# A two-block transformer kernel: the split weight rings whi and wlo placed 16 bytes lower in SBUF

## The chip, the cores and the metric

One core of a Trainium2 chip runs the whole program in one launch. The metric is the device time of that launch in microseconds (us). The kernel before was timed at 2585.36 us, the median of 3 runs (2585.33 to 2587.22).

## The reference

The reference computes two transformer blocks one after the other on 256 tokens of width 2048, in float32.

- First block: a position embedding is added to x; a modulation vector comes from silu(c) @ w_mod (2048 x 12288), also for a context; both x and the 256 context tokens are normalised, modulated and multiplied by w_in (2048 wide); gated linear attention runs in both directions, with the states of the context carried over; a 2-D Fourier mix runs beside it; both branches are read out (w_fourier_out, w_gla_out), gated and multiplied by w_out; then a squared-ReLU MLP, h @ w_mlp_in (2048 x 8192) and back by w_mlp_out.
- Second block: RMS norm, h @ w_in_2, three convolution and pooling mixers, w_out_2, a norm; then a gated convolution MLP with w_up_2 (2048 x 11264) and w_down_2 (5632 x 2048), and a last norm.

Nearly all arithmetic is in the matrix products with weights that come from HBM, some 540 MB in float32, each used once.

## The kernel before, in words

**Split products.** TensorE multiplies operands of type float32r. To keep float32 accuracy most weights w are split in two, whi (w rounded to float32r) and wlo (w minus whi), and so are the activations (hh and hl, mh and ml, ch and cl, dh and dl, oh and ol, yfh and yfl, all named "hi" and "lo" below). Each product of a 128 x 128 block of weights is three matmuls: hi times whi, hi times wlo, lo times whi.

**Staging.** SyncE loads weight slots of 128 x 2048 float32 (1 MB) into the ring `raw` (four slots, six while `raw2` is free). A slot gives two pieces of 128 x 1024. For each piece ScalarE copies raw to whi (`hi_piece`, L246, instruction at L254), VectorE subtracts to make wlo (`lo_piece`, L258, instruction at L263), and TensorE uses both. whi and wlo are rings of four pieces each; `STREAM` and `PIECE` give the order of slots and pieces, and semaphores count them: whi may be overwritten once `used` shows that TensorE is four pieces on, and TensorE waits for `lo_n`. The last two pieces of all go to `xh` and `xl` (128 x 2 x 1024 each), which lie elsewhere, so that they can be split before the ring is free.

**Two forms of a piece.** In `feature_piece` (L285, matmuls at L295, L297 and L299) the weights are the stationary operand, 128 x 128 at a time, and the moving operand is 256 tokens of an activation; a piece has 24 such matmuls. In `token_piece` (L304, matmuls at L315, L316 and L317) an activation block of 128 tokens is stationary and 512 columns of whi or wlo are moving; a piece has 12 matmuls, or 24 where the context is done with it. The last group of w_down_2 is written out at L2055 to L2057 in the same way; of its six pieces, the first four are in whi and wlo and the last two in xh and xl. `mm_lr` (L358, L367 to L369) has one piece with 64-column weights. Four groups at L352 use weights from raw without the split.

**Placement.** SBUF tensors lie one behind the other in each partition; an `overlay` gives several tensors the same region in turn. What matters for the change is where each operand begins, in bytes of a partition, modulo 128. Every matmul operand begins at a whole number of 512 bytes from the start of its tensor (256 in `mm_lr`), so these remainders hold for all of them.

| tensor | use in the matmuls | begins at, modulo 128 |
|---|---|---|
| whi | weights (feature), moving (token) | 16 |
| wlo | the same | 80 |
| hh, hl, mh, ml, ch, cl, oh, ol, yfh, yfl | moving (feature), stationary (token) | 32 |
| dh, dl | stationary (token, w_down_2) | 0 |
| xh, xl | moving (last two pieces) | 32 |
| raw, tmp | read by ScalarE and VectorE; raw is also the stationary operand at L352 | 0 |
| raw2 | as raw, for two slots of six while it is free | 32 |
| hf | moving at L352 | 32 |

hh begins at byte 109,472, mh at 142,240, oh at 191,904; hl, ml and ol, which follow them, at 125,856, 158,624 and 200,096. Each of the whi and wlo tensors has 16 columns (64 bytes) more than the ring needs; the ring begins 4 columns into it.

The lines that the diff touches are the two that allocate whi and wlo in `build`.

Of the kernel before, what the change touches and what calls it, by code (L numbers as in the profile page):

```python
# [4 lines left out]
P = 128  # L5
# [3 lines left out]
GC = 512  # L9
# [80 lines left out]
def build(nc, ins, out):  # L90
    f32, f32r, u32 = mybir.dt.float32, mybir.dt.float32r, mybir.dt.uint32
# [4 lines left out]
    with ctx:  # L96
        def sb(name, shape, dt=f32):
            return ctx.enter_context(nc.sbuf_tensor(name, shape, dt))
# [12 lines left out]


        raw = sb("raw", [P, NSLOT, 4 * GC])
        whi = sb("whi", [P, 8 * GC + 16], f32r)[:, 4:8 * GC + 4].rearrange("p (r n) -> p r n", r=4)
        wlo = sb("wlo", [P, 8 * GC + 16], f32r)[:, 4:8 * GC + 4].rearrange("p (r n) -> p r n", r=4)
        tmp = sb("tmp", [P, 2, 4 * NT])
        (mrow, cv, posc, macc, stage, _, posc2, sx, post) = overlay(
            "region_s", 8192,
# [2031 lines left out]
```

How the kernel before makes its waits and increments, by code:

```python
        def load(sp, st, name, slot, n=4, cols=4 * GC):  # L211
            for i in range(slot, slot + n):
                if PREV[st.k] is not None:
                    c = STREAM[PREV[st.k]]
                    before = STREAM[:PREV[st.k] + 1]
                    n_mod = before.count("m")
                    if c == "m" and n_mod <= EARLY:
                        sp.wait_ge(S["mod_used"], n_mod)
                    elif c == "m":
                        sp.wait_ge(S["mod_acc"], n_mod - EARLY)
                    elif c == "f":
                        sp.wait_ge(S["f_used"], before.count("f"))
                    else:
                        sp.wait_ge(S["lo_n"], 2 * before.count("d") + before.count("l"))
                sp.dma_start(raw_slot(st.k)[:, 0:cols], ins[name][i]).then_inc(raw_full[RING[st.k]], 16)
                st.k += 1
# [7 lines left out]
        def slot_in(eng, k):  # L235
            eng.wait_ge(raw_full[RING[k]], 16 * FILLS[k])
# [9 lines left out]
        def hi_piece(act, st):  # L246
            k, j = PIECE[st.p]
            if j == 0:
                slot_in(act, k)
            if st.p >= len(PIECE) - 2:
                act.wait_ge(S["fid_ok"], FT // 4)
            elif st.p >= 4:
                act.wait_ge(S["used"], st.p - 3)
            nc.scalar.activation(ring(whi, xh, st.p), raw_slot(k)[:, 2 * GC * j:2 * GC * (j + 1)], ACT.Copy)\
                .then_inc(S["hi_n"], 1)
            st.p += 1
# [24 lines left out]
        def group_done(eng, st):  # L281
            eng.wait_ge(S["used"], st.e)
```

## Time and profile before

| | us |
|---|---|
| median of 3 runs | 2585.36 |
| the profiled execution | 2586.47 |
| its span on the core | 2584.7 |
| TensorE busy in it | 2533.3 |
| VectorE busy | 1669.4 |
| ScalarE busy | 1141.4 |

The span is what the hardware profiler saw of the core's instructions; the execution's own time is 1.8 us longer, outside it. The profiled execution is 1.1 us above the median. Matmuls are pipelined: each lasts longer in the profile than the distance from its start to the start of the next, so what a matmul costs is read from starts, as first start and last start over the number between them, and not from the mean duration of one.

### The profile page before, as it was taken

To read this page: it belongs to the slowest core of one execution; us is meant where nothing else is said; L and a number is where in the kernel's file an instruction comes from. 1 tells how busy PE (TensorE), PEld (TensorE's weight loads), DVE (VectorE), ACT (ScalarE), POOL (GpSimd) and SP (SyncE) were. 2 spreads that over 40 slices of the span, in tenths; PEclk is the share of its full clock that TensorE was granted. 3 is DMA by queue.
4 is the path that set the end of the run, shared out by engine and by line. 5 is a ranking of instruction groups with operands and counts; after the bars stand their busy time and mean duration, and the time that the engine had idled before them with its cause. 6 is when DMAs were issued, how large, how long until landed. Compare 5 with 4: busy or idle time off the path is not lost.

```text
span 2584.7 us, 42715 instructions
## 1 busy us (share of the span) xinstructions
PE 2533.3 (98%) x18976; PEld 2379.1 (92%) x18976; DVE 1669.4 (65%) x2016; ACT 1141.4 (44%) x1311; POOL 11.2 (0%) x24
## 2 busy tenths in 40 slices
PE   6999999999998999999999999999999999999998
PEld 3688799999998999999999999999899889988997
DVE  5366666677787755555545579776667557764775
ACT  3422555544445434434434552054445444443554
POOL 0000000000000000000000000000000000000000
PEclk8999999999999999999999999999999999999999
DMA  9966565587875755555555555455455555555543
GB/s 401 371 241 231 213 225 198 212 300 289 303 288 195 289 184 196 184 192 194 184 193 193 183 181 178 147 180 177 149 181 196 195 182 193 192 184 194 186 175 128
DMA packets 77224, 547.90 MB, mean 212 GB/s; under 512 B 8848, under 2 KB 8976, under 8 KB 12272
## 3 DMA queue, kind: packets, MB, share of 16 engines
q1 hardware_dynamic: 74304, 533.53, 56.9%
q0 software_dynamic: 2448, 11.14, 1.1%
q8 instruction: 149, 2.44, 0.4%
q10 hardware_dynamic: 288, 0.50, 0.1%
q14 instruction: 35, 0.29, 0.0%
HBM read 539.90 MB, written 5.24 MB: 211 GB/s over the span
## 4 chain that ended last, share of the span: by engine, by line
PE 96%; DMA 1%; DVE 1%; ACT 1%; issue 1%; SPq 0%; DVEq 0%; ACTq 0%
PE acc L295 23%; PE acc L299 23%; PE acc L297 23%; PE acc L315 5%; PE acc L316 5%; PE acc L317 5%; PE acc L352 4%; DMA raw<-in_w_mod 1%; PE mp L382 1%; PE mp L315 1%; PE mp L317 1%; PE mp L316 1%; PE mp L441 0%; DVE macc L426 0%; PE mp L1857 0%
## 5 line engine op out<-in xcount | busy, mean ns | idle before, releaser
L263 DVE TENSOR_TENSOR wlo<-raw,whi 128x1024 fp32r<-128x1024 f32 x779 | 942.3, 1223 | 679.4 <-ACT whi L254 678.1
L254 ACT ACTIVATE whi<-raw 128x1024 fp32r<-128x1024 f32 x779 | 818.3, 1058 | 1180.9 <-PE acc L299 881.3
L295 PE MATMUL acc<-hh,whi 128*128 128x256 f32 x3360 | 940.1, 280 | 5.5 <-issue 5.5
L299 PE MATMUL acc<-hl,whi 128*128 128x256 f32 x3360 | 941.6, 280 | 0.0
L297 PE MATMUL acc<-hh,wlo 128*128 128x256 f32 x3360 | 934.7, 278 | 0.0
L295 PEld LDWEIGHTS acc<-hh,whi 128*128 128x128 f32 x3360 | 635.5, 189 | 10.6 <-issue 8.9
L299 PEld LDWEIGHTS acc<-hl,whi 128*128 128x128 f32 x3360 | 632.0, 188 | 0.0
L297 PEld LDWEIGHTS acc<-hh,wlo 128*128 128x128 f32 x3360 | 630.3, 188 | 0.5
L299 PE MATMUL acc<-ml,whi 128*128 128x256 f32 x1536 | 430.4, 280 | 0.0
L295 PE MATMUL acc<-mh,whi 128*128 128x256 f32 x1536 | 426.6, 278 | 0.0
L297 PE MATMUL acc<-mh,wlo 128*128 128x256 f32 x1536 | 426.5, 278 | 0.0
L295 PEld LDWEIGHTS acc<-mh,whi 128*128 128x128 f32 x1536 | 290.5, 189 | 0.3 <-issue 0.2
L299 PEld LDWEIGHTS acc<-ml,whi 128*128 128x128 f32 x1536 | 288.4, 188 | 0.0
L297 PEld LDWEIGHTS acc<-mh,wlo 128*128 128x128 f32 x1536 | 287.3, 187 | 0.1
L426 DVE SCALAR_TENSOR_TENSOR macc<-raw,csl,macc 128x512 f32<-128x512 f32 x240 | 180.2, 751 | 8.0
L316 PE MATMUL acc<-wlo,dh 128*128 128x512 f32 x328 | 129.9, 396 | 0.0
L317 PE MATMUL acc<-whi,dl 128*128 128x512 f32 x328 | 129.5, 395 | 0.0
L315 PE MATMUL acc<-whi,dh 128*128 128x512 f32 x328 | 129.4, 395 | 0.0
L352 PE MATMUL acc<-hf,raw 128*128 128x256 f32 x512 | 112.8, 383 | 4.1 <-ACT hf L991 4.1
L352 PEld LDWEIGHTS acc<-hf,raw 128*128 128x128 f32 x512 | 98.4, 192 | 18.0 <-issue 4.4
L1659 DVE SCALAR_TENSOR_TENSOR up<-um,par,up 128x255 f32<-128x255 f32 (+1 forms) x176 | 73.3, 479 | 25.3 <-ACT up L1014 24.5
L315 PE MATMUL acc<-whi,hh 128*128 128x512 f32 x192 | 79.5, 414 | 0.0
(332 smaller groups left out, 2213.1 us busy)
## 6 DMA issues: line engine op xcount, KB each, us to landing
raw<-in_w_in SPq DMA_DIRECT2D x98, 1024.0 KB, 4.9
raw<-in_w_mod SPq DMA_DIRECT2D x96, 1024.0 KB, 5.7
raw<-in_w_up SPq DMA_DIRECT2D x88, 1024.0 KB, 4.8
raw<-in_w_mlp_in SPq DMA_DIRECT2D x64, 1024.0 KB, 4.8
raw<-in_w_mlp_out SPq DMA_DIRECT2D x64, 1024.0 KB, 4.8
raw<-in_w_down SPq DMA_DIRECT2D x44, 1024.0 KB, 4.8
raw<-in_w_out SPq DMA_DIRECT2D x32, 1024.0 KB, 4.9
raw<-in_w_fourier_out SPq DMA_DIRECT2D x8, 1024.0 KB, 5.5
```

Of the source, the lines that this page charges most:

```text
L254: nc.scalar.activation(ring(whi, xh, st.p), raw_slot(k)[:, 2 * GC * j:2 * GC * (j + 1)], ACT.Copy)\
L263: nc.vector.tensor_tensor(ring(wlo, xl, st.p), raw_slot(k)[:, 2 * GC * j:2 * GC * (j + 1)], ring(whi, xh, st.p).bitcast(f32), ALU.subtract ...
L295: nc.tensor.matmul(dst, whi[:, r, cols], hi[:, kt, :], start=begin, stop=False, skip_group_check=True)
L297: nc.tensor.matmul(dst, wlo[:, r, cols], hi[:, kt, :], start=False, stop=False, skip_group_check=True)
L299: last = nc.tensor.matmul(dst, whi[:, r, cols], lo[:, kt, :], start=False, stop=kt == nkt - 1, skip_group_check=True)
L315: nc.tensor.matmul(dst, hi[:, kt, t0:t0 + P], whi[:, r, cols], start=kt == 0, stop=False)
L316: nc.tensor.matmul(dst, hi[:, kt, t0:t0 + P], wlo[:, r, cols], start=False, stop=False)
L317: last = nc.tensor.matmul(dst, lo[:, kt, t0:t0 + P], whi[:, r, cols], start=False, stop=kt == nkt - 1)
L352: last = nc.tensor.matmul(acc[i][:, t * NT:(t + 1) * NT], raw_slot(k)[:, j * GC + t * P:j * GC + (t + 1) * P], h[:, kt, :], start=kt == 0 ...
L382: last = nc.tensor.matmul(rows[32 * t:32 * t + 32, :], cv[:, 4 * s + t, :], raw_slot(k)[:, t * GC:(t + 1) * GC], start=s == 0, stop=s == 3)
L426: ins = nc.vector.scalar_tensor_tensor(macc[:, g % 2, :], part, csl[:, kt:kt + 1], macc[:, g % 2, :], ALU.mult, ALU.add)
L1659: last = nc.vector.scalar_tensor_tensor(y, um[:, t, 0:NT - sh], par[:, ds(col, 1)], y, ALU.mult, ALU.add)
```

## The change

Both rings begin at the start of their tensors in place of 16 bytes in. The tensors keep their sizes, so that everything else lies where it lay. No instruction, wait or transfer is added, removed or moved; whi begins at 0 and wlo at 64 modulo 128.

```diff
-        whi = sb("whi", [P, 8 * GC + 16], f32r)[:, 4:8 * GC + 4].rearrange("p (r n) -> p r n", r=4)
-        wlo = sb("wlo", [P, 8 * GC + 16], f32r)[:, 4:8 * GC + 4].rearrange("p (r n) -> p r n", r=4)
+        whi = sb("whi", [P, 8 * GC + 16], f32r)[:, 0:8 * GC].rearrange("p (r n) -> p r n", r=4)
+        wlo = sb("wlo", [P, 8 * GC + 16], f32r)[:, 0:8 * GC].rearrange("p (r n) -> p r n", r=4)
```

## Rows read from the trace of the kernel before

**Rows 1.** The page: busy us and share of each engine; chain by engine.
```profile
PE 2533.3 (98%) x18976; PEld 2379.1 (92%) x18976; DVE 1669.4 (65%) x2016; ACT 1141.4 (44%) x1311; POOL 11.2 (0%) x24
...
PE 96%; DMA 1%; DVE 1%; ACT 1%; issue 1%; SPq 0%; DVEq 0%; ACTq 0%
```
**Rows 2.** Waits, longest first: engine, waited for, total us, times, longest us.
```profile
ACT whi L254 <- PE acc L299: 881.3, 470, 83.0
DVE wlo L263 <- ACT whi L254: 678.1, 458, 8.8
```
**Rows 3.** Groups by form, TensorE: count, busy us and mean ns, idle before.
```profile
L299 PE MATMUL acc<-hl,whi 128*128 128x256 f32 x3360 | 941.6, 280 | 0.0
L299 PE MATMUL acc<-ml,whi 128*128 128x256 f32 x1536 | 430.4, 280 | 0.0
L299 PE MATMUL acc<-ol,whi 128*128 128x256 f32 x128 | 35.9, 280 | 0.0
L299 PE MATMUL acc<-yfl,whi 128*128 128x256 f32 x128 | 35.9, 280 | 0.0
L316 PE MATMUL acc<-wlo,dh 128*128 128x512 f32 x328 | 129.9, 396 | 0.0
L316 PE MATMUL acc<-wlo,hh 128*128 128x512 f32 x192 | 76.4, 398 | 0.0
L316 PE MATMUL mp<-wlo,ch 128*128 128x512 f32 x96 | 37.8, 394 | 0.0
```
**Rows 4.** Timeline, TensorE (start us, us, ...): the first MLP, first and last start.
```profile
910.62 0.36 PE L295 MATMUL acc<-mh,whi 128*128 128x256 f32 x1
...
1526.28 0.28 PE L299 MATMUL acc<-hl,whi 128*128 128x256 f32 x1
```
**Rows 5.** Timeline, TensorE, token form with dh, then feature form with hh.
```profile
2016.38 0.40 PE L315 MATMUL acc<-whi,dh 128*128 128x512 f32 x1
...
2105.47 0.40 PE L317 MATMUL acc<-whi,dl 128*128 128x512 f32 x1
2105.70 0.28 PE L295 MATMUL acc<-hh,whi 128*128 128x256 f32 x1
...
2283.10 0.28 PE L299 MATMUL acc<-hl,whi 128*128 128x256 f32 x1
```
**Rows 6.** Timeline, TensorE, token form with hh and ch, first and last.
```profile
122.81 0.47 PE L315 MATMUL acc<-whi,hh 128*128 128x512 f32 x1
...
200.73 0.39 PE L317 MATMUL mp<-whi,cl 128*128 128x512 f32 x1
```
**Rows 7.** Windows on TensorE: busy us, count, granted clock, DMA share, GB/s.
```profile
910.62:1526.28 615.66, 615.66 (x5330) 1.00 0.53 188
2016.38:2105.47 89.09, 89.09 (x386) 1.00 0.53 188
```
**Rows 8.** Timeline, TensorE, last group: pieces in xh, then whi, then xh.
```profile
2565.06 0.40 PE L2055 MATMUL acc<-xh,dh 128*128 128x512 f32 x1
...
2567.87 0.40 PE L2055 MATMUL acc<-whi,dh 128*128 128x512 f32 x1
...
2573.46 0.39 PE L2055 MATMUL acc<-xh,dh 128*128 128x512 f32 x1
...
2576.04 0.40 PE L2057 MATMUL acc<-xh,dl 128*128 128x512 f32 x1
```
**Rows 9.** Timeline, TensorE, the `mm_lr` piece, first and last start.
```profile
236.13 0.28 PE L367 MATMUL acc<-hh,whi 128*64 128x256 f32 x1
...
247.25 0.28 PE L369 MATMUL acc<-ch,wlo 128*64 128x256 f32 x1
```
**Rows 10.** The chain in order of time: start us, us, what (plain products, L352).
```profile
1579.96 82.88 PE acc L352 x384
```
**Rows 11.** Groups by form, ScalarE and VectorE, pieces of 128x1024.
```profile
L254 ACT ACTIVATE whi<-raw 128x1024 fp32r<-128x1024 f32 x779 | 818.3, 1058 | 1180.9 <-PE acc L299 881.3 <-PE acc L317 144.3 <-PE mp L317 62.5
L895 ACT ACTIVATE mh<-tmp 128x1024 fp32r<-128x1024 f32 x16 | 17.0, 1060 | 24.3 <-DVE tmp L1368 24.3
L254 ACT ACTIVATE xh<-raw 128x1024 fp32r<-128x1024 f32 x2 | 2.0, 1048 | 0.0
L263 DVE TENSOR_TENSOR wlo<-raw,whi 128x1024 fp32r<-128x1024 f32 x779 | 942.3, 1223 | 679.4 <-ACT whi L254 678.1
L1371 DVE TENSOR_TENSOR ml<-tmp,mh 128x1024 fp32r<-128x1024 f32 x16 | 19.6, 1225 | 18.0 <-ACT mh L895 18.0
```
**Rows 12.** The chain in order of time, two pieces among the gaps.
```profile
279.27 0.96 ACT whi L254
285.64 1.14 DVE wlo L263
```

## The prediction

> **What bounds the kernel now.** I read the page first: TensorE is busy 98% of the span, and the chain that ended last is 96% TensorE [rows 1]. The waits say the same from the other side: ScalarE waits 881.3 us for TensorE before it may overwrite a piece of whi, and VectorE waits for ScalarE, not for data [rows 2]. So the only thing that can move the time by more than a few us is what a matmul costs in a row without gaps. The groups by form show that nearly all matmuls use whi or wlo, with no idle time before them [rows 3]. There are 15,456 of 256 moving columns in the feature form (5,152 at each of L295, L297 and L299: 3,360 + 1,536 + 128 + 128), 96 in mm_lr, and 1,920 of 512 columns in the token form (616 at each of three lines, as 328 + 192 + 96, and 72 in the last group, 24 of which read xh or xl).
>
> What one costs I read from starts in the timeline. Feature form in the first block's MLP, hh and mh in turn: 222 pieces of 24, so 5,328 matmuls, start from 910.62 to 1526.28 us; 615.66 us over 5,327 is 115.6 ns [rows 4]. With hh alone, 64 pieces: 177.40 us over 1,535, 115.6 ns [rows 5]. Token form with dh, 32 pieces of 12: 89.09 us over 383, 232.6 ns [rows 5]; with hh and ch, 336 matmuls: 77.92 us over 335, 232.6 ns [rows 6]. The granted clock is 1.00 (2.4 GHz) in these stretches [rows 7], so the array itself needs 256 / 2.4 = 106.7 ns and 512 / 2.4 = 213.3 ns. The rest, 8.9 and 19.3 ns, is a loss on every matmul, 15,456 x 8.9 + 1,920 x 19.3 = 175 us in all. The plain float32 products at L352, two passes each, take 82.88 / 384 = 215.8 ns a pass of 256 columns, twice 106.7 and only 2.5 more [rows 10]: where a column goes in every second cycle hardly anything is lost. The loss grows with the columns, not with the number of matmuls, and is there only at full rate. That looks like the reading of the moving operand being held up, perhaps by the weight load that runs at the same time, and this change moves one of the two streams in every one of these matmuls.
>
> **The change part by part.** Nothing is issued, removed or waited for anew. Three kinds of accesses begin 16 bytes lower.
>
> ScalarE's writes and VectorE's reads and writes. A piece costs 1058 ns on ScalarE with whi at 16, 1060 with mh at 32, 1048 with xh at 32; on VectorE 1223 with raw at 0 and whi at 16, 1225 with tmp at 0 and mh at 32 [rows 11]. I bound the edit at 12 ns a piece either way, at most 779 x 12 ns = 9.3 us on ScalarE, which waits 881.3 us for TensorE alone, so it is hidden [rows 2]. Uncovered it is in a few places only, as at 279 and 285 us, where a piece is waited for by the scans [rows 12]; some ten pieces by 12 ns are 0.1 us. I take 0.
>
> whi and wlo as moving operands (1,896 token matmuls that change). The nearest rows are the last group, the one place where the same matmuls run with the ring in two places: with whi and wlo at 16 and 80, 24 matmuls in 2573.46 - 2567.87 = 5.59 us, 232.9 ns; with xh and xl at 32, 12 in 2.81 us and 11 distances in 2.58 us, together 5.39 / 23 = 234.3 ns [rows 8]. That is 1.4 ns more. With 23 distances read to 0.01 us it is uncertain by about half of itself. What differs is the distance between the two streams. With dh at 0, whi at 16 is 16 modulo 32 away from the weights and xh is 0 modulo 32 away. Now all other rows: feature form, moving 32 and weights 16 or 80, distance 16 modulo 32; token form with hh, 16 modulo 32 too; with dh, 16 again. All of these run at the same two rates, to 0.1 ns, whatever the tensor [rows 4 to 6]. The only pair at distance 0 modulo 32 and full rate is the slower one. The change puts every pair there: 32 against 0 or 64 in the feature form, 0 or 64 against 32 or 0 in the token form. So 1,896 x 1.4 ns = 2.7 us slower.
>
> whi and wlo as weights (15,456 matmuls, and 96 of mm_lr). No row shows them at a distance of 0 modulo 32 at full rate. From below: nothing, or a gain as large as the loss taken next, since no row excludes that a start at 0 helps a load. From above: if a matmul pays 1.4 ns whatever its columns, 15,552 x 1.4 = 21.8 us. mm_lr shows by chance the same: its loads have another shape and its matmuls start 11.12 us / 95 = 117.1 ns apart, 1.5 ns over the usual 115.6 [rows 9], which gives 23 us. If the loss grows with the columns, as the 8.9 and 19.3 ns above do, it is half, 0.7 ns, and 15,552 x 0.7 = 10.9 us. I take the half, since the present loss follows the columns in just that way.
>
> Sum: 10.9 + 2.7 = 13.6 us. On the profiled execution's own time, 2586.5 + 13.6 = 2600.1 us; that execution is 1.1 us over the median of the runs shown, so 2599 us for the median, 0.5% slower. TensorE has no cover for this: each ns goes into the end, and ScalarE and VectorE only wait longer.
>
> Two rules of the Trainium skill speak against this. The row first: token matmuls run at 232.6 ns with stationary blocks at 0 as at 32 modulo 128 [rows 5, 6]. The page "SBUF — State Buffer", section "Door 1: The DMA port swizzle", says that the memory is read in lines of 16 bytes and that full rate needs at least two accesses to a line. By it 0 and 16 are both starts of a line, four float32 columns lie in each, and nothing changes. Its sections on the engine ports, and "TensorE: Matmul & The Clock Gate", section "Part 2: What happens when you issue a matmul", give TensorE two independent read ports, so that a load takes nothing from a running matmul. By that rule a distance between the streams could not matter at all and the sum would be 0. The trace neither proves nor refutes this: the 8.9 ns of loss have no cause in either page, and the 1.4 ns of rows 8 go against the second rule, weakly.
>
> **The rivals.**
>
> *No change (25%).* What holds up the moving operand has nothing to do with start bytes. For it: hl, ml and ol lie at 125,856, 158,624 and 200,096, and their matmuls last 280 ns each [rows 3], two rates equal to 0.1 ns [rows 4 to 6], and stationary blocks at 0 and 32 alike. Against it: rows 8, and that all these equal rows share one distance modulo 32. It gives 2585.4 us. That the change does not do what it says belongs here: both rings stay inside tensors of the same size, so nothing else can move.
>
> *Slower by much more (8%).* The two streams, once in step, hold each other up on some matmuls by as much again as each loses now. The place is the feature form; with a quarter of its matmuls the price is 3,864 x 8.9 = 34 us, 2619 us. For it speaks only that the present loss is that large; against it that rows 8, the same distance, show 1.4 ns and not more.
>
> *Faster (19%).* The loss comes from starts inside a 32-byte stretch: 16 and 80 modulo 128 are the only operands here that do not begin at a multiple of 32, and L352, without the loss, has both of its operands at such multiples (0 and 32) [rows 10]. The place is the load of whi or wlo in each feature matmul, and the price is what is now lost at such a start. If that were the whole of 8.9 ns, 15,456 of them would give 138 us; but in the token form whi moves and dh is loaded, and in the last group xh at 32 moves with dh at 0, no such start anywhere, and still 234.3 ns pass, 21 over the array's 213.3 [rows 8]. So the loss is not made by such starts, and only a small part can be. I price it as the measured difference with its sign turned, 13.6 us, and 2572 us; it decides against my forecast as soon as a feature matmul costs under 115.2 ns.
>
> **How the numbers follow.** Chances: slower, as forecast or more, 56% (48 and 8); no change 25%; faster 19%. A measurement of this kernel can tell about 0.2% from no change, that is 5 us, or 0.33 ns on each of the feature matmuls. The likeliest case's own range is from 2591 (0.35 ns a matmul) to 2611 us (the price that does not depend on columns, 21.8 + 2.7 = 24.5 us, with 1 us over). The whole range is 2576 to 2622 us: it takes in no change, most of the faster case, and the larger loss of 34 us. It leaves out some 9% below and 9% above.
>
> **What would show it.** In the profile after, matmuls of L295 to L299 should start 116.3 ns apart and not 115.6 in the long stretch of the MLP (5,327 distances in about 619.5 us in place of 615.7), and those of L315 to L317 some 234 ns apart in place of 232.6. In the last group, whi and xh should then cost the same. ScalarE's and VectorE's pieces stay at 1058 and 1223 ns within 12 ns; ScalarE's wait for TensorE grows by about the same 10 us. It is wrong if the feature rate stays at 115.6 (no change), if it falls below 115.2, or if the time moves at other lines than those that read whi and wlo; and the step from 512 to 256 columns is wrong by itself if the token form moves by 1.4 ns and the feature form by another amount than 0.7.

## The result, and the profile after

The changed kernel takes 2615.38 us (median of 4 runs, 2614.07 to 2616.56) where the kernel before, timed beside it, takes 2585.35 us (median of 4): a ratio of 1.0117, 95% interval 1.0104 to 1.0129. It is 30 us slower. The direction was forecast, the size was not: 13.6 us and 2599 us were worked out, and the measured time lies some 70% of the way from there to the upper end of the range, 2622 us. The profiled executions differ by 27.6 us (2614.07 against 2586.47), and so do their spans (2612.3 against 2584.7).

The page and the waits of the changed kernel look like those of before [rows 1, 2]. TensorE is busy 27.0 us longer, ScalarE waits 23 us longer for it:

```profile
PE 2560.3 (98%) x18976; PEld 2407.1 (92%) x18976; DVE 1670.1 (64%) x2016; ACT 1140.6 (44%) x1311; POOL 11.2 (0%) x24
...
ACT whi L254 <- PE acc L299: 904.4, 487, 83.1
DVE wlo L263 <- ACT whi L254: 702.5, 464, 8.9
```

The groups of pieces show that ScalarE and VectorE pay nothing: 1057 and 1223 ns against 1058 and 1223 [rows 11].

```profile
L263 DVE TENSOR_TENSOR wlo<-raw,whi 128x1024 fp32r<-128x1024 f32 x779 | 943.0, 1223 | 704.3 <-ACT whi L254 702.5
L254 ACT ACTIVATE whi<-raw 128x1024 fp32r<-128x1024 f32 x779 | 817.4, 1057 | 1211.8 <-PE acc L299 904.4 <-PE acc L317 142.8 <-PE mp L317 63.1
```

The mean durations of the matmuls would mislead: 279 ns at L299 with hl, where it was 280 [rows 3]. The distances between starts in the timeline of TensorE tell the cost. First the MLP (to hold against rows 4), then dh and hh (rows 5), then hh and ch (rows 6), then mm_lr (rows 9):

```profile
917.50 0.36 PE L295 MATMUL acc<-mh,whi 128*128 128x256 f32 x1
...
1544.98 0.28 PE L299 MATMUL acc<-hl,whi 128*128 128x256 f32 x1
...
2039.68 0.39 PE L315 MATMUL acc<-whi,dh 128*128 128x512 f32 x1
...
2128.19 0.40 PE L317 MATMUL acc<-whi,dl 128*128 128x512 f32 x1
2128.43 0.28 PE L295 MATMUL acc<-hh,whi 128*128 128x256 f32 x1
...
2309.22 0.28 PE L299 MATMUL acc<-hl,whi 128*128 128x256 f32 x1
...
122.66 0.48 PE L315 MATMUL acc<-whi,hh 128*128 128x512 f32 x1
...
201.03 0.40 PE L317 MATMUL mp<-whi,cl 128*128 128x512 f32 x1
...
236.64 0.28 PE L367 MATMUL acc<-hh,whi 128*64 128x256 f32 x1
...
247.83 0.28 PE L369 MATMUL acc<-ch,wlo 128*64 128x256 f32 x1
```

| stretch | distances | before, ns | after, ns |
|---|---|---|---|
| feature form, MLP | 5,327 | 115.6 | 627.48 / 5,327 = 117.8 |
| feature form, hh (w_up_2, middle) | 1,535 | 115.6 | 180.79 / 1,535 = 117.8 |
| token form, dh | 383 | 232.6 | 88.51 / 383 = 231.1 |
| token form, hh and ch | 335 | 232.6 | 78.37 / 335 = 233.9 |
| mm_lr | 95 | 117.1 | 11.19 / 95 = 117.8 |

The granted clock is 1.00 in each of these stretches after, as it was before [rows 7].

So a feature matmul costs 2.2 ns more, and the token form gains in one place what it loses in another. 2.2 ns on 15,456 matmuls would be 34 us, and the feature form lost 27.8. Half of the missing 6 us (1,344 x 2.2 ns = 3.0 us) are in a stretch of the kernel before that my prediction had no row of, the first one of w_up_2 (before, then after):

```profile
1857.90 0.47 PE L295 MATMUL acc<-hh,whi 128*128 128x256 f32 x1
...
2016.26 0.28 PE L299 MATMUL acc<-hl,whi 128*128 128x256 f32 x1
```
```profile
1881.19 0.47 PE L295 MATMUL acc<-hh,whi 128*128 128x256 f32 x1
...
2039.56 0.28 PE L299 MATMUL acc<-hl,whi 128*128 128x256 f32 x1
```

1,343 distances in 158.36 us before and in 158.37 after, 117.9 ns both times. The kernel before ran here, at a granted clock of 1.00 and with the same addresses and the same instructions as in the w_up_2 stretch that starts 90 us after this one ends, at the changed kernel's rate. Another 1.1 us are in the 192 matmuls after a pause near 790 us, which took 24.63 us before, at a mean granted clock of 0.89, and 23.96 after, at 0.94, where 0.4 more were due; 1.1 us are in the four stretches between 517 and 715 us, which lost 1.5 to 1.8 ns a matmul; the rest is in short stretches. Over all stretches of the feature form the distances add up to 1793.9 us before and 1821.7 after, 27.8 us more, where the whole span is 27.6 us longer: all else nearly cancels.

Read one by one, the distances (the trace has starts in ns) repeat. Before, the three matmuls of a triple stand 114, 113 and 119 ns apart, in the slow stretch at 1858 us nearly all of them 117 to 119; after, 116, 119 and 118. I call such a repeating pattern a rhythm. The last group, where the prediction expected whi and xh to cost the same after the change, shows that they do not:

```profile
2592.75 0.39 PE L2055 MATMUL acc<-xh,dh 128*128 128x512 f32 x1
...
2595.56 0.39 PE L2055 MATMUL acc<-whi,dh 128*128 128x512 f32 x1
...
2601.11 0.39 PE L2055 MATMUL acc<-xh,dh 128*128 128x512 f32 x1
...
2603.67 0.40 PE L2057 MATMUL acc<-xh,dl 128*128 128x512 f32 x1
```

With whi and wlo at 0 and 64 it is 5.55 / 24 = 231.2 ns, with xh and xl, which did not move, (2.81 + 2.56) / 23 = 233.5 ns. Both now lie 0 modulo 32 from dh, and yet they are 2.3 ns apart, where it was 1.4 with different distances [rows 8].

### The profile page after: what moved, and what is told of

Same layout as the page of the kernel before. It is cut to its first block, busy times and chain, and to the rows that moved or that the text cites. A ratio compares the mean times of both kernels' runs of the same rounds, so it can differ in the third digit from the quotient of the medians.

```text
span 2612.3 us, 42715 instructions
## 1 busy us (share of the span) xinstructions
PE 2560.3 (98%) x18976; PEld 2407.1 (92%) x18976; DVE 1670.1 (64%) x2016; ACT 1140.6 (44%) x1311; POOL 11.2 (0%) x24
## 4 chain that ended last, share of the span: by engine, by line
PE 96%; DMA 1%; DVE 1%; ACT 1%; issue 1%; SPq 0%; DVEq 0%; ACTq 0%
PE acc L299 23%; PE acc L295 23%; PE acc L297 23%; PE acc L315 5%; PE acc L316 5%; PE acc L317 5%; PE acc L352 4%; DMA raw<-in_w_mod 1%; PE mp L382 1%; PE mp L316 1%; PE mp L315 1%; PE mp L317 1%; PE mp L441 0%; DVE macc L426 0%; PE mp L1857 0%
## 5 line engine op out<-in xcount | busy, mean ns | idle before, releaser
L263 DVE TENSOR_TENSOR wlo<-raw,whi 128x1024 fp32r<-128x1024 f32 x779 | 943.0, 1223 | 704.3 <-ACT whi L254 702.5
L254 ACT ACTIVATE whi<-raw 128x1024 fp32r<-128x1024 f32 x779 | 817.4, 1057 | 1211.8 <-PE acc L299 904.4
L299 PE MATMUL acc<-hl,whi 128*128 128x256 f32 x3360 | 938.0, 279 | 0.0
L299 PEld LDWEIGHTS acc<-hl,whi 128*128 128x128 f32 x3360 | 642.0, 191 | 0.0
L295 PEld LDWEIGHTS acc<-hh,whi 128*128 128x128 f32 x3360 | 629.2, 187 | 10.2 <-issue 8.9
L299 PE MATMUL acc<-ml,whi 128*128 128x256 f32 x1536 | 428.6, 279 | 0.0
L299 PEld LDWEIGHTS acc<-ml,whi 128*128 128x128 f32 x1536 | 293.3, 191 | 0.0
L352 PE MATMUL acc<-hf,raw 128*128 128x256 f32 x512 | 113.8, 386 | 4.1 <-ACT hf L991 4.1
L352 PEld LDWEIGHTS acc<-hf,raw 128*128 128x128 f32 x512 | 99.1, 194 | 18.4 <-issue 4.4
```

The costliest lines, as they stand in the source:

```text
L254: nc.scalar.activation(ring(whi, xh, st.p), raw_slot(k)[:, 2 * GC * j:2 * GC * (j + 1)], ACT.Copy)\
L263: nc.vector.tensor_tensor(ring(wlo, xl, st.p), raw_slot(k)[:, 2 * GC * j:2 * GC * (j + 1)], ring(whi, xh, st.p).bitcast(f32), ALU.subtract ...
L295: nc.tensor.matmul(dst, whi[:, r, cols], hi[:, kt, :], start=begin, stop=False, skip_group_check=True)
L299: last = nc.tensor.matmul(dst, whi[:, r, cols], lo[:, kt, :], start=False, stop=kt == nkt - 1, skip_group_check=True)
L352: last = nc.tensor.matmul(acc[i][:, t * NT:(t + 1) * NT], raw_slot(k)[:, j * GC + t * P:j * GC + (t + 1) * P], h[:, kt, :], start=kt == 0 ...
```

## The experiments

Twelve kernels ran. Five of them, m1 to m5, hold only matmuls on one core with a few tensors, so that the starts of every operand can be chosen; their rates are worked out from starts, and the first matmuls of each case, in which the pattern is still settling, are left out. The very first case of each needs more care. It begins with 13 to 27 matmuls that start 213 ns apart, 256 columns at the lower clock level of 1.2 GHz, and fall to about 118 ns in one step. In m3_pair 11 distances from 25.66 to 28.01 us are 213 ns each and 18 from 28.83 to 30.98 us are 119.6; the trace's record of the granted clock begins, at 1.00, at 28.8 us:

```profile
25.66 0.84 PE L18 MATMUL acc<-act_hi,ring_hi 128*128 128x256 f32 x3
...
28.01 0.63 PE L18 MATMUL acc<-act_hi,ring_hi 128*128 128x256 f32 x2
...
28.83 0.52 PE L18 MATMUL acc<-act_hi,ring_hi 128*128 128x256 f32 x3
...
30.98 0.52 PE L18 MATMUL acc<-act_hi,ring_hi 128*128 128x256 f32 x3
```

A mean over all of such a case shows the clock and not the placement; the rates below are those at 1.00.

**m1_map: matmuls alone, starts modulo 128.**

```
for w in range(0, 128, 16):        # start of whi; wlo 64 on
    for m in range(0, 128, 16):    # start of the activations
        feature form, 72 matmuls   (later: token form, 36)
```

> Only matmuls, nothing else of the computation (the output is not the reference's): the feature form (three matmuls of 256 columns for each 128 x 128 block: hi by whi, hi by wlo, lo by whi; 72 for each case) and the token form (three of 512 columns, 36 for each case), for each of 8 starts of the ring (whi at w = 0, 16 ... 112 modulo 128, wlo always 64 on) and each of 8 starts of the activations (m = 0, 16 ... 112). No other engine is at work. Theory A (the distance m - w modulo 32 decides): the 64 cases of a form fall into two groups only, distance 16 modulo 32 at about 115.6 ns a feature matmul and distance 0 modulo 32 at about 117.8; token 232.6 and the others in one group. Theory B (the start of the ring alone decides, whatever the activations): all 8 cases of one w are equal, w = 16 at 115.6, w = 0 at 117.8. Theory C (the pair of starts decides, with a longer period than 32): more than two levels. All three: m = 32 with w = 16 gives 115.6 and with w = 0 gives 117.8, or the cause is not in the matmuls themselves but in the other engines' accesses to the rings (theory D: then all cases are equal).

About half of the feature cases ran at 117.8 ns, the others from 115.5 to 120.1. So theories A, B and D fall and C stands: there are many levels, with no other engine at work, and neither the distance modulo 32 nor one start decides. w = 0 with m = 32 gave 117.8 as in the changed kernel, but w = 16 with m = 32 also gave 117.8 and not 115.6. I took that to mean that remainders modulo 128 are not enough. It does not show it: in this kernel's layout the case starts at 144, 208 and 160 modulo 256, as the kernel before does, and the next map gives another reason.

**One ring moved, and both moved on** (columns of 4 bytes; the kernel before has 4 and 4, the changed one 0 and 0):

```diff
 e_whi_only:  whi [:, 0:8 * GC]          wlo [:, 4:8 * GC + 4]
 e_wlo_only:  whi [:, 4:8 * GC + 4]      wlo [:, 0:8 * GC]
 e_plus32:    whi [:, 8:8 * GC + 8]      wlo [:, 8:8 * GC + 8]
```

> whi at 0, wlo stays at 80. In each triple of the feature form whi is loaded twice and wlo once. Theory A: two of three matmuls have the slow distance; two thirds of the feature part, 2 x 5152 x 3.3 ns: 2585 + 0.67 x 34 = 2608 us with the token form between its two values. Theory B: the same if the cost is that of a load. Rival (the pair whi and wlo matters by its own distance, 64 modulo 128 before and after): 48 instead of 64 gives something of its own, outside 2585 to 2615 us.

> wlo at 64, whi stays at 16. Theory A and B: a third of the cost: 2585 + 0.33 x 34 = 2596 us. Rival (whi and wlo matter by their own distance): outside 2585 to 2615 us.

> whi at 32 and wlo at 96: 32 bytes on from the changed kernel, 16 on from the kernel before. Theory A (distance modulo 32): as the changed kernel, 2615 us, feature 117.8 ns. Theory B with a period of 32: the same. With a period of 64 or 128 (theory C): a value of its own, 2570 to 2640 us.

Measured, one run each beside 2589.3 us of the kernel before: 2615.8, 2624.8 and 2617.4 us. The MLP's feature matmuls were 117.8, 118.5 and 117.8 ns apart. The parts of the change do not add: either half costs the feature form as much as the whole or more (1822.0 and 1833.3 us in all its stretches, against 1821.7 with both moved), and moving wlo alone is the slowest. A cost per load of whi or wlo, as my sum had it, cannot give that. Both times lie outside 2585 to 2615 us, the range that the rival in the two expectations named (the distance between whi and wlo counts), the first by 0.8 us only. e_plus32 agrees with theory A by its number only, since m1_map refutes it.

**m2_map512: the kernel's own starts modulo 512.** 104 feature cases and 64 token cases, among them (whi, wlo, activations) = (144, 208, 416), the kernel before, and (128, 192, 416), the changed one.

> Only matmuls again (the output is not the reference's), in the kernel's two forms, 72 or 36 for each case, but now whi, wlo and the activations start where they do in the kernel modulo 512 bytes and not modulo 128. Theory C512 (the starts of all streams modulo 512 decide): whi 144, wlo 208, activations 416 gives the kernel before's 115.6 ns; whi 128, wlo 192 the changed kernel's 117.8; 128 and 208 gives 117.8 and 144 and 192 gives 118.5, as the two runs with one ring moved had; 160 and 224 gives 117.8; token form with activations at 0: 232.6 for whi at 144, 231.1 for 128, 235.4 for 160. Rival theory D (the absolute place in SBUF or the other engines' accesses decide): these cases do not come out at those values, as the first map's case at 16 and 32 modulo 128 did not (117.8 in place of 115.6).

(128, 192) gave 117.8, (160, 224) 117.8, (144, 192) 118.6, (128, 208) 117.8, and the token form with dh 232.6, 231.1 and 235.4 ns once settled: seven of the eight values named, within 0.1 ns, so the operands' places make the rates, with no other engine at work. The token map repeats with a period of 256 bytes. The eighth value came out both ways, in one and the same kernel: (144, 208, 416) ran at 117.8 ns in three sweeps and at 115.5 in the fourth, where another case stood ahead of it. Its rows, in the first sweep and then in the fourth, 41 distances each:

```profile
105.31 0.28 PE L22 MATMUL acc<-act_hi,ring_hi 128*128 128x256 f32 x1
...
110.14 0.28 PE L24 MATMUL acc<-act_lo,ring_hi 128*128 128x256 f32 x1
...
879.25 0.28 PE L22 MATMUL acc<-act_hi,ring_hi 128*128 128x256 f32 x1
...
883.99 0.28 PE L24 MATMUL acc<-act_lo,ring_hi 128*128 128x256 f32 x1
```

4.83 and 4.74 us, 117.8 and 115.6 ns. One placement has more than one rhythm, as the stretch at 1858 us of the kernel before had said. A step of 4 bytes matters as well: with both rings at 128 + 4 the case ran at 120.0.

**m3_pair: one block of weights, one moving operand.**

> Only matmuls, one block of weights and one moving operand over and over (the output is not the reference's): 128 weight columns by 256 moving columns, 40 for each of 32 distances between the starts of the two (0 to 496 bytes by 16), with the weights at 0 and again at 16; then 128 by 512, 64 by 256, 32 by 256 and 32 by 512, each over the 32 distances. Theory E (the weight load and the moving operand, read at the same time, hold each other up): the loss over 106.7 ns depends on the distance, and it shrinks with the columns of the load, to about a quarter with 32. Theory F (the loss is the moving operand's own, by its start or by its rate): the loss is the same for 32 columns as for 128, near 9 ns for 256 and 19 for 512, and flat over the distance.

Time between the starts of two matmuls, ns (the last 18 of a case, 9 with 512 columns), over 32 distances in bytes from 0 to 496 by 16:

| weight columns by moving columns | lowest | mean | highest | at the lowest |
|---|---|---|---|---|
| 128 by 256, weights at 0 | 113.3 | 118.0 | 120.0 | 4 of 32 |
| 128 by 256, weights at 16 | 113.3 | 118.7 | 123.3 | 2 of 32 |
| 64 by 256 | 113.3 | 116.8 | 120.0 | 5 of 32 |
| 32 by 256 | 113.3 | 114.8 | 117.8 | 19 of 32 |
| 128 by 512 | 226.7 | 232.0 | 234.3 | 4 of 32 |
| 32 by 512 | 226.7 | 231.4 | 240.2 | 6 of 32 |

The case at distance 16, weights at 0, with 128 and then with 32 columns of weights, 33 distances each, 3.91 / 33 = 118.5 and 3.75 / 33 = 113.6 ns:

```profile
31.83 0.52 PE L18 MATMUL acc<-act_hi,ring_hi 128*128 128x256 f32 x3
...
35.74 0.52 PE L18 MATMUL acc<-act_hi,ring_hi 128*128 128x256 f32 x3
...
662.08 0.51 PE L18 MATMUL acc<-act_hi,ring_hi 128*32 128x256 f32 x3
...
665.83 0.50 PE L18 MATMUL acc<-act_hi,ring_hi 128*32 128x256 f32 x3
```

Neither theory wins alone. With 256 moving columns the load does hold up the moving operand (E): the rate depends on where the two start, and with the smaller load 26 of the 32 cases are faster, 19 of them at the floor. With 512 it does not hold: a load of 32 columns is slower in 14 cases, up to 240.2 ns. And a floor stays that no distance and no small load removes (F): 113.3 = 106.7 + 6.7 ns, and 226.7 = 213.3 + 13.3. I count the loss in stalls of 6.7 ns. 115.6 is 106.7 + 4/3 x 6.7, 117.8 has 5/3, 118.5 has 16/9, 120.0 has 2; in the token form 232.6 has 26/9 over 213.3 and 231.1 has 24/9. So a triple of the kernel before loses four such units and one of the changed kernel five. This is arithmetic on the measured rates; that the hardware stalls by whole units of 6.7 ns is not shown. Steps of ninths fit nearly any rate, and single distances do not fit: at distance 32 every matmul stands 116 or 117 ns from the last, mean 116.7, which is one and a half.

Here the Trainium skill can be held against numbers. Its page "TensorE: Matmul & The Clock Gate", section "Part 2: What happens when you issue a matmul", says that a load takes no read bandwidth from a running matmul. For float32r the table above shows matmuls of 256 columns slowed by a load at most distances, 118.0 ns in the mean with 128 columns of weights and 114.8 with 32; that it is the read bandwidth which they share is not shown. And the lines of 16 bytes of "SBUF — State Buffer", section "Door 1: The DMA port swizzle", do not foretell that a step of 16 bytes, from one line's start to the next, moves a rate from 115.6 to 117.8.

**m4_grid: whi by wlo, 256 placements.**

> Only matmuls in the feature form (the output is not the reference's), 60 for each case: whi at each of 16 starts and wlo at each of 16 starts modulo 256 bytes, activations at 160 modulo 256 as in the kernel. Theory G (three streams in lock step: each case settles into a repeating pattern of whole stalls of 6.7 ns, chosen by all three starts): rates are 106.7 ns plus 6.7 times a simple fraction (4/3 stalls give 115.6, 5/3 give 117.8, 2 give 120.0), with no rule for one ring alone: changing wlo alone changes the rate by row and column in no additive way. Theory A' (one ring's distance to the activations is enough): whole rows or whole columns of the grid are equal.

Theory G held against A': no row or column is constant. Four of the 16 rows (whi down, wlo across, activations at 160 modulo 256), ns, each case entered once:

```
whi\wlo     0    16    32    48    64    80    96   112   128   144   160   176   192   208   224   240
   96   117.8 117.9 115.5 117.7 117.8 117.8 117.8 117.8 117.8 117.8 117.9 117.8 117.8 117.8 118.9 117.8
  128   118.8 117.8 117.8 118.9 117.8 116.6 118.9 117.8 116.7 117.8 117.0 118.7 117.8 117.8 119.3 117.8
  144   116.7 118.4 117.8 117.9 118.3 117.8 117.8 120.1 117.8 120.1 117.9 117.8 118.5 115.5 117.0 120.0
  224   118.9 118.9 118.2 117.7 117.9 117.0 113.3 117.8 117.8 117.8 117.8 117.8 117.8 116.7 113.3 117.8
```

117.8 is the common rate, in about half of the 256 cases; the slowest has 124.6. The kernel before (144, 208) sits in one of four cases of 256 at 115.5 or 115.6; only (224, 96) and (224, 224) have 113.3. The other 250 run at 116.6 or more, so nearly any move from the kernel before's place costs something.

**Three placements taken into the whole kernel.**

```diff
 e_wlo_at_16:   wlo = sb("wlo", [P, 8 * GC + 80], f32r)[:, 20:8 * GC + 20]     (whi as before)
 e_plus4bytes:  whi [:, 1:8 * GC + 1]       wlo [:, 1:8 * GC + 1]
 e_plus48:      whi [:, 12:8 * GC + 12]     wlo [:, 12:8 * GC + 12]
```

> The kernel before with whi where it was and wlo 64 bytes further on (208 to 272 modulo 512; its tensor made 256 bytes longer, so that all behind it moves by 256 bytes). Theory G from the second map, where whi 144 and wlo 272 ran at 115.5 ns at once: 2585 us, within 4 us, the token form apart. Theory A (distance modulo 32 alone): the same as before too. Theory 'the two rings must be 64 apart': slower, as the two runs with one ring moved (2616 and 2625 us).

> Both rings 4 bytes on from the changed kernel (132 and 196 modulo 512). Theory G with the second map: 120.0 ns for each feature matmul, two stalls each, so 2585 + 15,456 x 4.4 ns = 2653 us. Theory 'lines of 16 bytes: a start inside a line costs, and 0 and 16 are alike': slower than the changed kernel too, but the kernel before and the changed one would be alike, which they are not. Theory A: distance 28 modulo 32, undefined.

> Both rings 48 bytes on from the changed kernel (176 and 240 modulo 512), distance to the activations again 16 modulo 32. Theory A (distance modulo 32): 2585 us, as before. Theory G with the second map (118.3 ns a feature matmul, token form 230.3 and 231.7): 2585 + 15,456 x 2.7 ns - 3 us = 2624 us.

One run each beside 2583.94 us: 2619.71, 2638.28 and 2619.52 us. e_plus48 came close to its number (118.35 ns in the MLP for 118.3; 2624 were expected) and has the distance 16 modulo 32 of the kernel before: theory A is dead in the whole kernel too. e_wlo_at_16 missed by 35 us: 115.5 ns was expected, and it ran at 118.5 in the MLP and 117.8 later. The two maps differ on this very place (whi 144, wlo 16 modulo 256): 115.5 in m2_map512, 118.4 in m4_grid. e_plus4bytes missed by 15 us for the same reason, and its timeline shows it in the plainest way, the MLP and then w_up_2:

```profile
924.29 0.36 PE L295 MATMUL acc<-mh,whi 128*128 128x256 f32 x1
...
1551.77 0.28 PE L299 MATMUL acc<-hl,whi 128*128 128x256 f32 x1
...
2143.79 0.28 PE L295 MATMUL acc<-hh,whi 128*128 128x256 f32 x1
...
2327.96 0.28 PE L299 MATMUL acc<-hl,whi 128*128 128x256 f32 x1
```

627.48 / 5,327 = 117.8 ns and 184.17 / 1,535 = 120.0 ns, with the same code, the same starts modulo 256 and a granted clock of 1.00 in both. A map in which each case is entered once tells which rhythms there are, not which one a kernel will fall into.

**m5_leads: each placement entered 12 times.** One matmul of 32 to 448 columns stands ahead of each entry.

> Only matmuls in the feature form (the output is not the reference's): 12 placements, each entered 12 times, 60 matmuls each time, with one matmul of 32 to 448 columns on other addresses ahead, so that the rhythm is entered at 12 phases. Theory G with more than one stable rhythm: the kernel before's placement (144, 208, activations 416) settles at 115.6 in some entries and at 117.8 in others; the changed kernel's (128, 192, 416) at 117.8 in all; 132 and 196 at 117.8 in some and 120.0 in others; 224 and 224 at 113.3 in most. With all three streams moved together by 32 or 64 bytes each placement has the same rates as unmoved; moved by 16 or 48, other ones. Rival (one placement, one rate): all 12 entries of a placement are equal.

| whi, wlo, activations | ns, and number of entries |
|---|---|
| 144, 208, 416 (before) | 115.6: 12 |
| the same, all three + 32 | 115.6: 11; 117.8: 1 |
| the same, all three + 64 | 115.6: 10; 117.8: 2 |
| the same, all three + 16 or + 48 | 118.1 to 118.5: 24 |
| 128, 192, 416 (changed) | 117.8: 12 |
| the same, all three + 32 or + 64 | 117.8: 24 |
| the same, all three + 16 or + 48 | 120.0: 24 |
| 132, 196, 416 | 120.0: 12 |
| 224, 224, 416 | 113.3: 10; 117.8: 2 |

The last 27 distances of the second entry at the kernel before's place, at the changed kernel's, and at 224 and 224:

```profile
36.13 0.28 PE L20 MATMUL acc<-act_lo,ring_hi 128*128 128x256 f32 x1
...
39.25 0.28 PE L20 MATMUL acc<-act_lo,ring_hi 128*128 128x256 f32 x1
...
465.11 0.28 PE L20 MATMUL acc<-act_lo,ring_hi 128*128 128x256 f32 x1
...
468.29 0.28 PE L20 MATMUL acc<-act_lo,ring_hi 128*128 128x256 f32 x1
...
986.99 0.28 PE L20 MATMUL acc<-act_lo,ring_hi 128*128 128x256 f32 x1
...
990.05 0.28 PE L20 MATMUL acc<-act_lo,ring_hi 128*128 128x256 f32 x1
```

3.12, 3.18 and 3.06 us over 27. The changed kernel's place has only the 117.8 ns rhythm, in 36 of 36 entries; that of before has a faster one that it nearly always finds. Distances alone do not fix the rate: all three moved together by 32 bytes keep it, by 16 they do not. Not all came as expected: 132 and 196 showed only 120.0 in 12 entries, though the whole kernel ran at 117.8 there for the 627 us of the MLP.

**e_224_224: the best place, in the whole kernel.**

```diff
-        whi = sb("whi", [P, 8 * GC + 16], f32r)[:, 4:8 * GC + 4]...
-        wlo = sb("wlo", [P, 8 * GC + 16], f32r)[:, 4:8 * GC + 4]...
+        whi = sb("whi", [P, 8 * GC + 80], f32r)[:, 24:8 * GC + 24]...
+        wlo = sb("wlo", [P, 8 * GC + 16], f32r)[:, 8:8 * GC + 8]...
```

> The kernel before with whi and wlo both at 224 modulo 256, 64 bytes after the activations (the tensor of whi made 256 bytes longer, so that all behind keeps its place modulo 256). In the grid this place ran at 113.3 ns, one stall a matmul, from the second matmul on. Theory G: the feature form at 113.3 to 113.6 ns, 15,456 x 2.2 ns = 34 us under the kernel before, 2551 us with the token form within 5 us of its own; any rhythm of 117.8 ns entered in the kernel after a pause would show as a time between 2551 and 2620 us. Rival (the kernel before is as fast as such placements get in the whole kernel, the grid's best is chance): 2585 us or more.

2560.96 us, median of 4 runs, against 2587.21 of the kernel before on the same chip: 0.9905, 95% interval 0.9888 to 0.9921. It is faster than both kernels, and its rings start at the same place modulo 256, so the theory that they must be 64 bytes apart falls as well. The MLP, and then the first w_in_2 group (432 matmuls):

```profile
904.02 0.36 PE L295 MATMUL acc<-mh,whi 128*128 128x256 f32 x1
...
1507.85 0.28 PE L299 MATMUL acc<-hl,whi 128*128 128x256 f32 x1
...
1511.23 0.47 PE L295 MATMUL acc<-hh,whi 128*128 128x256 f32 x1
...
1562.18 0.28 PE L299 MATMUL acc<-hl,whi 128*128 128x256 f32 x1
```

603.83 / 5,327 = 113.4 ns, and 50.95 / 431 = 118.2 ns: the second rhythm, in stretches that hold some 17% of the feature matmuls, and the main reason why only 26 of the expected 34 us came.

## Why the prediction was half right

- **What bounds the kernel: right.** The whole difference is in the distance of matmul starts with no gap, 27.8 us in the feature form alone. ScalarE's and VectorE's pieces stayed as they were; the waits that grew are ScalarE's for TensorE, 23 us, and VectorE's for ScalarE behind it, 24 us.
- **The cause, one stream against the other: right in kind, wrong in its rule.** The loss does depend on where the two streams start (m3_pair). "Distance 16 modulo 32 is fast, 0 is slow" fell at once: the token form with dh got 1.5 ns faster where 1.4 ns slower was forecast, e_plus48 has distance 16 and costs 118.35 ns, and e_224_224 has distance 0 modulo 32 and is the fastest of all. I had taken the stretches of rows 4 to 6, all at one rate, for as many tests; they all shared one arrangement.
- **The direction: right, but by luck.** It was argued from that rule, which is false. Slower was likely for another reason: m4_grid has 250 of 256 placements slower than the kernel before's own, so almost any move would have cost.
- **whi and wlo as moving operands, 2.7 us: wrong.** hh and ch lost 1.4 ns as forecast, dh gained 1.5; with 864 and some 1,030 matmuls of each they cancel. The 1.4 ns of rows 8 were measured rightly, as a property of that place only.
- **whi and wlo as weights, 10.9 us: the step that failed in size.** I took 0.7 ns a matmul, half of 1.4, because the loss over 106.7 grew with the columns. It was 2.2 ns, three times as much, 27.8 us in place of 10.9. The token form with dh moved by 1.5 ns the other way in the same change, so one form gives neither the sign nor the size of the other, and scaling a small difference by columns had no ground. The bound that I set from above, 1.4 ns, was too low as well; w_up_2 in e_plus4bytes has 4.4 ns over the kernel before, 120.0 for 115.6.
- **The term that I had no eye for, -3 us and more:** the kernel before was already in the slow rhythm for a tenth of its feature matmuls. One row at 1858 us would have shown 117.9 ns beside 115.6, at equal addresses, and with it a second rate 2.3 ns off, and that addresses do not fix the rate.
- **No change** fell with the result, and with it the reading that starts at 0 and at 16 are alike. **Faster** was wrong for this change, though its idea that another start could be faster was right.

## What to carry to other kernels

When float32r matmuls run back to back, measure the distance of their starts against columns / 2.4 GHz, once the granted clock is 1.00. Here 6.7 ns or more were always over on 256 columns, and the start bytes of stationary and moving operands, down to 4 bytes, changed how much. Search such placements with a small kernel of matmuls alone, enter each place at many phases, and confirm in the whole kernel, for one placement can have two rates. Do not derive a rule from stretches that all share one arrangement, nor attribute a slower stretch to its code before looking for the same code at another rate.

## What the runs showed of the hardware that was not expected

- One float32r matmul of 256 columns never came below 113.3 ns in sustained running in any of these maps, 6.7 over the 106.7 of the array, while the passes of plain float32 at L352 still take 215.8 ns [rows 10] in every kernel.
- A placement, a code and a granted clock of 1.00 do not fix the rate: 117.8 and 120.0 ns in one execution of e_plus4bytes, 115.6 and 117.9 in the kernel before.
- Beside 512 moving columns a small load is hardly cheaper: 231.4 ns in the mean over 32 distances with 32 columns of weights, 232.0 with 128, and the slowest case, 240.2 ns, has the small load.
- Open: what the loss is, whether it has a unit, and what chooses the rhythm in the whole kernel. The loss does not need the other engines, since the maps show it with none at work; whether their accesses or the semaphores of each piece push the rhythm over was not tried.
